# Two blocks with mixtures of experts on one core: the last 16 rows of one weight unit in each tile are sent as two transfers of 8 rows

## The reference

```python
h = h + hybrid_mixer(rmsnorm(h, norm_mix[l]), w_in[l], ...)
h = h + expert_choice_ffn(rmsnorm(h, norm_ffn[l]), w_router[l], w_gate, w_up, w_down)
# in the ffn: 16 experts of 1024 x 1024, each takes the 32 tokens that rate it highest
a = jnp.einsum('becd,edf->becf', xe, w_gate)
u = jnp.einsum('becd,edf->becf', xe, w_up)
ye = jnp.einsum('becf,efd->becd', jax.nn.silu(a) * u, w_down)
```

```python
hid = silu(einsum('td,edf->tef', t, w_gate[gi])) * einsum('td,edf->tef', t, w_up[gi]) * combine
out = out + jnp.einsum('tef,efd->td', hid, w_down[gi])
```

## Time and profile before

| what | value |
|---|---|
| median of 3 runs | 2142.53 us (2142.21 to 2148.26) |
| the profiled execution's own time | 2147.99 us |
| its span, first to last instruction | 2146.2 us |
| PE busy | 1917.2 us, 89% of the span |
| mean granted clock of TensorE | 0.985 |
| moved by DMA | 748.52 MB, mean 349 GB/s |
| share of 16 DMA engines' time by the kernel's own queue (q1) | 85.3% |

### The profile page before, as it was taken

The page is one execution under the profiler, slowest core; times in us unless marked ns, Lnnn a source line. Parts: engine busy times, 40 slices in busy tenths (PEclk is TensorE's granted clock), DMA queues, the critical chain, the costliest instruction groups (busy, mean ns, idle before and its releaser), DMA issues.

```text
span 2146.2 us, 32065 instructions
## 1 busy us (share of the span) xinstructions
PE 1917.2 (89%) x14254; PEld 1185.0 (55%) x14254; DVE 645.6 (30%) x992; ACT 545.4 (25%) x837; POOL 0.2 (0%) x4
## 2 busy tenths in 40 slices
PE   9999998787878999999898988889999998878796
PEld 8988832121312898872333433359999644444443
DVE  4476500000000548641431111057657300000001
ACT  4366300000000347530201222033544211011111
POOL 0000000000000000000000000000000000000000
PEclk9999999999999999999999999999999999999999
DMA  9734999999999962699999999974426999999996
GB/s 355 263 129 167 397 418 428 428 428 428 428 428 415 369 228 80 239 377 421 426 423 419 421 424 421 428 271 157 157 80 233 416 425 428 429 423 427 424 426 267
DMA packets 123028, 748.52 MB, mean 349 GB/s; under 512 B 6288, under 2 KB 27152, under 8 KB 83344
## 3 DMA queue, kind: packets, MB, share of 16 engines
q1 hardware_dynamic: 122896, 746.52, 85.3%
HBM read 745.45 MB, written 1.05 MB: 348 GB/s over the span
## 4 chain that ended last, share of the span: by engine, by line
PE 55%; DMA 37%; DVE 4%; ACT 2%; issue 1%; SPq 0%; DVEq 0%; ACTq 0%
PE bank L802 19%; DMA ring<-w_expert_up 12%; PE bank L893 10%; DMA ring<-w_expert_down 10%; PE bank L946 8%; DMA ring<-w_expert_gate 5%; PE bank L805 5%; DMA ring<-moe_w_up 5%; DMA ring<-moe_w_down 3%; DMA arena<-moe_w_up 2%; PE bank L924 2%; PE bank L829 1%; PE bank L1097 1%; PE bank L1118 1%; PE bank L1170 1%
## 5 line engine op out<-in xcount | busy, mean ns | idle before, releaser
L893 PE MATMUL bank<-ring,arena 128*32 128x512 f32 (+1 forms) x3232 | 518.2, 509 | 85.1 <-DMA ring<-w_expert_up 39.4
L893 PEld LDWEIGHTS bank<-ring,arena 128*32 128x32 f32 x3232 | 164.8, 109 | 407.4 <-issue 210.9
L946 PE MATMUL bank<-ring,arena 128*32 128x512 f32 x1280 | 279.3, 606 | 48.2 <-DMA ring<-w_expert_down 38.5
L802 PE MATMUL bank<-arena_parts,ring_parts 128*128 128x256 f32 x1296 | 293.9, 283 | 0.0
L802 PEld LDWEIGHTS bank<-arena_parts,ring_parts 128*128 128x128 f32 x1296 | 218.6, 189 | 6.6 <-ACT arena_parts L1722 2.3
L946 PEld LDWEIGHTS bank<-ring,arena 128*32 128x32 f32 x1280 | 68.8, 111 | 238.9 <-issue 171.0
L1722 ACT ACTIVATE arena<-bank 128x512 f32<-128x512 f32 (+1 forms) x142 | 73.7, 544 | 452.3 <-PE bank L908 216.3
L2265 DVE TENSOR_TENSOR arena<-arena,bank 128x512 f32<-128x512 f32 x24 | 15.8, 685 | 553.7 <-PE bank L893 553.7
L802 PE MATMUL bank<-extra_parts,ring_parts 128*128 128x256 f32 x512 | 144.2, 282 | 0.0
L802 PE MATMUL bank<-ring_parts 128*128 128x256 f32 x688 | 132.4, 284 | 1.8 <-DVE ring_parts L2694 0.9
L802 PEld LDWEIGHTS bank<-ring_parts 128*128 128x128 f32 x688 | 109.0, 189 | 4.0 <-DVE ring_parts L2694 1.2
(11 more groups left out here) (385 smaller groups left out, 2391.1 us busy)
## 6 DMA issues: line engine op xcount, KB each, us to landing
ring<-w_expert_down SPq DMA_DIRECT2D x62, 2048.0 KB, 24.0
ring<-w_expert_gate SPq DMA_DIRECT2D x58, 2048.0 KB, 23.4
ring<-w_expert_up SPq DMA_DIRECT2D x54, 2048.0 KB, 25.6
ring<-w_in SPq DMA_DIRECT2D x32, 2048.0 KB, 11.7
ring<-moe_w_up SPq DMA_DIRECT2D x24, 2048.0 KB, 28.3
ring<-moe_w_gate SPq DMA_DIRECT2D x20, 2048.0 KB, 37.9
arena<-moe_w_down SPq DMA_DIRECT2D x16, 2048.0 KB, 34.0
ring<-ada_w SPq DMA_DIRECT2D x12, 2048.0 KB, 16.9
```

The costliest lines, as they stand in the source:

```text
L802: last = pe.matmul(out[:, n * S:(n + 1) * S], w[:, k, n * P:(n + 1) * P], x[:, k, :], start=first, stop=final)
L893: last = pe.matmul(to[own_rows(half, e)].rearrange("p (q c) -> p q c", c=own), x_slots[:, c, 32 * e:32 * e + 32], w[:, k, half], start=c = ...
L946: last = pe.matmul(banks[4 + e // PAIRS][own_rows(half, e), :].rearrange("p (x d) -> p x d", x=2), hidT[:, e // PAIRS * own + f % own, own ...
```

## The change

One unit of each tile of the first block's layers (unit 20, of `w_expert_down`) and one unit of each round of the second block (unit 8 of its second tile, `moe_w_down`) goes as three transfers. Rows 112 to 119 and rows 120 to 127 are issued first, as transfers of 8 rows that share a semaphore of their own, and rows 0 to 111 follow with the slot's semaphore. PE waits for both semaphores ahead of that unit's products. That makes 8 uneven units in the first block and 4 in the second. The bytes are the same.

```diff
+UNEVEN1 = 20
+UNEVEN2 = 8
+EVEN_ROWS = 112
+FEW_ROWS = 8
...
+                        if u == UNEVEN1:
+                            pe.wait_ge(few_rows_loaded, (layer * TILES1 + t + 1) * (P - EVEN_ROWS) // FEW_ROWS * 16)
...
+                            if h and u == UNEVEN2:
+                                pe.wait_ge(few_rows2_loaded, (p * (TILES2 // 2) + t + 1) * ((P - EVEN_ROWS) // FEW_ROWS * 16))
...
+                if few is not None:
+                    for p0 in range(EVEN_ROWS, P, FEW_ROWS):
+                        part = slice(p0, p0 + FEW_ROWS)
+                        sp.dma_start(to[part], rows[part, :, first:first + cols]).then_inc(few, 16)
+                    load(at, to[0:EVEN_ROWS], rows[0:EVEN_ROWS, :, first:first + cols], loaded)
+                    return
                 load(at, to[:, :, begin:cols], rows[:, :, first + begin:first + cols], loaded)
...
+                                     few=few_rows_loaded if u == UNEVEN1 else None)
...
+                                 few=few_rows2_loaded if (h, u) == (1, UNEVEN2) else None)
```

More of the change, by code:

```diff
@@ L667, in build @@
         last_half2_loaded = sem("second_last_unit_first_half_loaded")
+        few_rows_loaded = sem("uneven_unit_few_rows_loaded")
+        few_rows2_loaded = sem("second_uneven_unit_few_rows_loaded")
         spare2_loaded = [sem(f"spare_unit_loaded_{i}") for i in range(SPARE2)]
@@ L3049, in load_cols, with load_expert_unit @@
                 load(at, dst, src[:, bass.ds(c0, cols)].rearrange("(k p) n -> p k n", p=P))
-            def load_expert_unit(at, u, gate, up, down, t, f_width, slot=slot, loaded=lambda at: unit_loaded[at], shared=0, half=None):
+            def load_expert_unit(at, u, gate, up, down, t, f_width, slot=slot, loaded=lambda at: unit_loaded[at], shared=0, half=None, few=None):
                 n_in, n_out = unit_counts(f_width)
@@ L3099, in load_tile_unit @@
                     last = (t, u) == (TILES1 - 1, UNITS1_TILE - 1)
-                    load_expert_unit(SLOT_OF[layer][unit], u, *experts, t, FE, half=last_half_loaded if last else None)
+                    load_expert_unit(SLOT_OF[layer][unit], u, *experts, t, FE, half=last_half_loaded if last else None,
+                                     few=few_rows_loaded if u == UNEVEN1 else None)
                 order = list(enumerate(HEAD_ORDER))
@@ L3206, in load_unit2 @@
                 load_expert_unit(SLOT2_OF[h, u], u, *experts, t * 2 + h, FE2, slot2, loaded2, 0 if h else SHARED2,
-                                 half=last_half2_loaded if (h, u) == (1, UNITS2_TILE - 1) else None)
+                                 half=last_half2_loaded if (h, u) == (1, UNITS2_TILE - 1) else None,
+                                 few=few_rows2_loaded if (h, u) == (1, UNEVEN2) else None)
             def free2(h, u, t, **back):
```

## The result

| what | before | after |
|---|---|---|
| median, range | 2145.4 us (2142.21 to 2150.77, 4 runs) | 2275.97 us (2275.66 to 2276.78, 4 runs) |
| the profiled execution's span | 2146.2 us | 2273.8 us |
| mean granted clock of TensorE | 0.985 | 0.959 |

The change makes the kernel slower: the ratio is 1.06 with a 95% interval of 1.0584 to 1.0616. That is 130.6 us, or 10.9 us for each of the 12 uneven units. The forecast was 3 us less, 2139.5 us. The median before has a fourth run in it that the 2142.53 us of the prediction did not have.

The account below looks back on a forecast made before the run. It took three DMA-bound expert streams, ended by their latest engines, to set the time. Gains of 2.45 (second block) + 0.3 + 0.3 (layers) made 3 us less than 2142.53: 2139.5 us, range 2135 to 2151.

Parts of the forecast that it names:

- Rows: At each uneven unit eight engines carry 9 rows, the others 7, at 0.61 us per row: 2.45 us shift per stream.
- The pieces collide: Rival: writes of a piece's neighbouring rows get in each other's way, 3.67 us per unit; 2183 or mildly 2149.5; chance 0.14.
- hard case: Full collision of the pieces in all three streams: 12 + 14 + 14 = 40 us slower, 2183 us.
- most of it may be avoided: Engines reach their rows up to 3 us apart, so perhaps a quarter of the collision remains: 2149.5 us.
- Which eight: The eight engines with 9 rows are taken to be the early half, those not fetching instructions; called the weakest step.
- the plateaus: DMA share near one half at stream ends, read as eight early and eight late engines, gaps about 5 and 3 us.
- The wrong half: Rival: the eight with 9 rows include late, instruction-fetching engines; each stream 2.45 us later, 2149.9 us; chance 0.14.
- a shift between halves: At the second block's end no long half plateau; share falls to 0 within some 4 us, ending 2.45 earlier.
- The bound: Three expert streams bound by DMA: time is the number of units times 4.89 us, PE waiting for the last engine.
- More transfers: Two more transfers per uneven unit, with SP's issues and PE's second wait, add nothing; at most 0.8 us per stream.
- The sign to look for: PE's starts around an uneven unit more than a fraction over 4.89 us apart would mean the pieces collide.

Follow-up runs that it names:

- Experiment 1: Changed kernel with only the 112 rows moved, rows 112 to 127 left out: 2220.35 us against 2144.99 before the change, ratio 1.0348.
- experiment 2: Changed kernel with only the two pieces of 8 rows moved, rows 0 to 111 left out: 2153.06 us against 2144.99 before the change, ratio 1.0024.
- Experiment 8: Kernel before, units whole, plus two transfers of 8 rows x 16 bytes into their own tile ahead of each of 12 units: 2146.81 us against 2147.66.
- experiments 3: Changed kernel, but the pieces take every second row (112, 114, ... 126 and 113, 115, ... 127): 2270.37 us, ratio 1.0581 to the kernel before.
- 7: Kernel before, with the 12 units as two halves by rows, 0 to 63 and 64 to 127: 2258.02 us against 2146.49, ratio 1.0519.
- 10 to 12: Only two 8-row pieces of each of the 12 units moved, rows 4, 2 or 16 apart: 2105.86, 2146.15, 2139.23 us; before, 2147.66, 2147.66, 2146.71.
- experiment 13: Kernel before, with the 12 units as their 64 even and 64 odd rows: 2148.03 us against 2146.71, ratio 1.0008.
- Experiment 4: Changed kernel, but the pieces read rows 16 apart in memory and write them to the same 16 slot rows: 2273.82 us, ratio 1.0598 to before.
- experiment 12: Only two 8-row pieces of each of the 12 units moved, rows 0, 16, ... 112 and 1, 17, ... 113: 2139.23 us against 2146.71 before.

## Why the prediction was wrong

**The failed step: "Rows".** It said that an engine carries 8 rows of a unit in 4.89 us, so "a row costs an engine 0.61 us", and took this for the 112 rows and the pieces alike. The rows of before show that price for transfers of all 128 rows only, as the earlier trace rows do. At the first uneven unit of the change a packet of one row takes 1.16 us while the 112 rows run and 2.3 while the pieces do; over all 12 units the slow packets have a median of 1.1 to 1.2 us. Experiment 1 puts 83 us on the first and experiment 2 59 us on the second. No case of the prediction had a cost for the 112 rows, which look like an almost whole unit; they were the larger part.

**"The pieces collide"** was the rival nearest to what happened, with a chance of 0.14, and its hard case stood outside the range. It had neighbouring rows in each other's way, but only those of the pieces. Its price was 3.67 us per unit on eight engines, less the slack of those engines, 40 us in all. The pieces cost 59 us. Slack of eight engines is no cover, because the slow packets are on all of them: at 118 GB/s with a share of 1.00, whole units' rows are slow too. The argument that "most of it may be avoided", since engines reach their rows up to 3 us apart, isn't borne out. Nothing was avoided, and the delay per unit is largest at the end of each stream, in the second block 8 us at the first uneven unit and 16 at the fourth. That fits engines that drift apart and are still on one transfer when others are on the next, but no run varied the drift. That whole units run at 428 GB/s was cited against a collision, with the right reason why it isn't evidence (each engine has its own partitions) right behind it; the reason should have been followed to "then a unit of 112 rows may lose that".

**The size per unit isn't fully explained.** Seven rows at the measured 1.16 us instead of 0.61 are 3.9 us for the 112 rows, and four rows in a row at one port instead of one are 1.8 us for the pieces, together 5.7 of 10.9. All slow packets together are 9.5 us per unit; in experiment 1 they are 6.6 of its 6.9, in experiment 2 3.8 of its 5.0. So most of the rest lies in slow packets of the transfers around the uneven unit. They last for 10 us at the first unit with the 112 rows alone and for 18 with the change; why they last so long is open. PE's lower clock isn't part of it at the first unit: the DMA share is 0.94 to 1.14 from 315 to 340, so no engine waited for PE to free a slot.

**"Which eight"**, called the weakest step, was wrong as well. Experiment 8 shows it, since its small transfers land on eight engines right behind a unit's rows. These are the events of the semaphores in its trace, us, for the last two small transfers of the second block and for a whole unit near it (by its last engine, the others before it):

```
two transfers of 8 rows: 2100.70 2100.88 2101.07 2101.29 2101.41 2101.60 2101.82 2102.00
                         2102.18 2102.37 2103.16 2103.36 2107.00 2107.15 2107.20 2107.36
whole unit, last 2117.93: -7.57 -7.26 -7.20 -6.86 -6.79 -6.51 -6.12 -5.09
                          -1.34 -1.33 -1.19 -1.15 -0.93 -0.23 -0.20 0.00
```

The whole unit shows two sets of eight engines, 4 to 7 us apart, as the plateaus of the earlier trace rows suggested. The small transfers come in pairs, so eight engines take both, as the prediction took it. The Trainium skill, page "DMA: Bandwidth & Descriptors", section "Why a DMA increments its semaphore by 16 and not by 1", gives 8 rows eight engines too, and this trace agrees. But six of the eight are early and two are late. The two late ones are 6.3 and 6.5 us behind the first, while the last engine of all is 7.57 behind. With 2.45 us more of rows they would have become the last. So without any collision the change would have lost an estimated 1.4 us here (6.5 + 2.45 - 7.57) and not gained 2.45: the rival "The wrong half", in a milder form. At the last uneven unit of both layers it is six and two as well.

The windows at the end of the changed kernel's second block say the same:

```profile
2247.00:2248.00 1.00, 1.00 (x10) 0.31 (x6) 0.00 (x0) 0.00 (x0) 0.00 (x0) 1.00 0.91 385
2248.00:2249.00 1.00, 1.00 (x8) 0.26 (x6) 0.00 (x0) 0.00 (x0) 0.00 (x0) 1.00 0.60 254
2249.00:2250.00 1.00, 1.00 (x6) 0.11 (x2) 0.00 (x0) 0.00 (x0) 0.00 (x0) 1.00 0.37 156
2250.00:2251.00 1.00, 0.23 (x2) 0.00 (x0) 0.00 (x0) 0.60 (x1) 0.00 (x0) 1.00 0.19 82
...
2253.00:2254.00 1.00, 1.00 (x8) 0.29 (x8) 0.00 (x0) 0.00 (x0) 0.00 (x0) 1.00 0.14 57
2254.00:2255.00 1.00, 1.00 (x10) 0.36 (x10) 0.00 (x0) 0.00 (x0) 0.00 (x0) 1.00 0.08 33
2255.00:2256.00 1.00, 1.00 (x12) 0.31 (x8) 0.00 (x0) 0.00 (x0) 0.00 (x0) 1.00 0.04 16
```

The plateau at one half of the earlier trace rows is gone, as forecast for a shift between halves. But after it a tail of one to three engines (0.19 to 0.04) runs on for 6 us, and from the share's 0.9 to 0 it takes 9 us as against 8 before, where the forecast had some 4. The engines were held up at the uneven units, so the plateau's end is no proof of the shift.

**What was right.** The bound: the three streams set the time, and nearly all of the 127.6 us came around the uneven units. "More transfers" cost nothing, nor did SP's issues and PE's second wait: experiment 8 has all of these at 0.9995. The sign to look for was also named: a step in PE's starts around an uneven unit that is longer than 4.89. At the first one it is 13.3 us, from 322.53 to 335.80.

**What stays open.** Shown is that the split by neighbouring rows makes the engines' packets slow, and that neither the number of transfers, nor their size, nor PE's second wait, nor the uneven load does it. That shared ports of the slot are the reason fits experiments 3, 4, 7 and 10 to 12 and needs an assumption on the dealing for the 112 rows and for experiment 13. A pattern of the reads in memory as the reason isn't excluded. Experiment 4 changed the pieces' reads from neighbours to 16 apart, and pieces with reads 16 apart are slow in experiment 12 as well; no run moved 64 or 112 rows to other places of the slot than those of their reads.

No kernel here beats the one before. The two splits that cost nothing, by columns and by even and odd rows, leave the engines' loads as they are; the one that moved load without the row split cost 33 us.

## What to carry to other kernels

- A transfer into all 128 partitions that runs at the full rate says nothing of one into a part of them. Before rows are cut, ask which partitions are written at the same time; cut by columns, or take rows spread over all 128, and measure a transfer of the new shape by itself.
- A DMA share near 1 with a falling rate beside it is a sign that single packets take longer. The share alone looks like a kernel that is well fed.
- An edit meant to shift 2.45 us between engines needs to know first which engines take the rows. A tiny transfer ahead of a unit shows it at no cost that could be measured (0.9995).

## What the runs showed of the hardware that wasn't expected

- 112 of 128 neighbouring rows go at half the rate: packets of 16 KB take mostly 1.1 to 1.2 us instead of 0.61, on all engines. With two halves of 64 neighbouring rows they take 1.1 to 1.8.
- 64 even rows and then 64 odd ones go at the full rate (2148.03 us against 2146.71).
- While PE waited 9.64 us for the uneven unit its clock fell to 0.50, and the next 16 products took 5.00 us; before it, at full clock, 3.63. PE's busy time rose from 1917.2 to 1956.2 us for the same 14,254 products.
- Engines that take a transfer of 8 rows are neither the early nor the late eight: at the last uneven unit of each stream they are six early and two late ones.
